# Tokens of a mixture-of-experts kernel gathered in 1 KB quarters and turned by VectorE in 32x32 blocks instead of by TensorE

## The reference

```python
DM, HID, EXPERTS, TOP_K = 1024, 512, 32, 2
x2 = rms_norm(h, ffn_norm[layer])                     # 512 x 1024
gp, gi = top_k(softmax(x2 @ w_r1 + b_r1), 1)          # one of 4 groups
ev, ei = top_k(fine logits of that group, 2)          # two of its 8 experts
gates = gp * softmax(ev)
for e in experts:                                     # w_gate, w_up: 1024 x 512, w_down: 512 x 1024
    y = (silu(x2[rows of e] @ w_gate[e]) * (x2[rows of e] @ w_up[e])) @ w_down[e]
    out[rows of e] += gate * y
h = h + out
```

## Time and profile before

| | us |
|---|---|
| median of 3 executions | 1716.42 (1715.44 to 1754.85) |
| profiled execution | 1716.88 |
| its span in the trace | 1715.0 |
| PE busy | 1654.8 (96%) |
| DVE busy | 743.6 (43%) |
| ACT busy | 327.6 (19%) |
| POOL busy | 76.7 (4%) |
| DMA queue 1, the weights | 455.11 MB, 67.7% of 16 engines' span |
| DMA queue 0, issued by POOL | 8.40 MB, 1.7% |

### The profile page before, as it was taken

How to read it: one execution, slowest core, us unless ns; L and a number is a source line. 1 busy time by engine, 2 the same in 40 slices (tenths; PEclk the granted TensorE clock), 3 DMA queues, 4 the chain that set the end, 5 groups by cost and what they waited for, 6 DMA issues and landing times.

```text
span 1715.0 us, 24253 instructions
## 1 busy us (share of the span) xinstructions
PE 1654.8 (96%) x10112; PEld 1088.4 (63%) x10119; DVE 743.6 (43%) x1281; ACT 327.6 (19%) x545; POOL 76.7 (4%) x76
## 2 busy tenths in 40 slices
PE   8999998999999999989999999999999999999998
PEld 6876686555555555547787787878655555555554
DVE  4899744333333333244453444445433333333333
ACT  4134621101001010123221222222100100000002
POOL 0030001000000000000000000000100000000000
PEclk9999999999999999999999999999999999999999
DMA  8212138999999999994222122127699999999995
GB/s 299 99 56 92 58 147 332 400 401 403 395 409 406 399 402 406 408 367 148 71 77 98 50 99 99 53 99 313 230 395 404 407 406 409 409 402 400 401 404 238
DMA packets 109553, 475.29 MB, mean 277 GB/s; under 512 B 10752, under 2 KB 23040, under 8 KB 76544
## 3 DMA queue, kind: packets, MB, share of 16 engines
q1 hardware_dynamic: 101120, 455.11, 67.7%
q0 software_dynamic: 5248, 8.40, 1.7%
q10 hardware_dynamic: 3072, 10.18, 1.5%
HBM read 476.27 MB, written 6.29 MB: 281 GB/s over the span
## 4 chain that ended last, share of the span: by engine, by line
PE 86%; DVE 8%; DMA 2%; issue 2%; ACT 1%; SPq 1%; DVEq 0%; POOLq 0%; ACTq 0%
PE psum L927 25%; PE psum L951 12%; PE psum L842 9%; PE psum L843 9%; PE psum L844 9%; PE psum L1038 8%; DVE h L2083 2%; PE psum L918 2%; PE psum L1336 2%; DVE xs L1747 2%; PE psum L936 2%; DMA raw<-in_odd_w_in 1%; PE psum L942 1%; DVE w_lo L666 1%; PE psum L1226 1%
## 5 line engine op out<-in xcount | busy, mean ns | idle before, releaser
L2083 DVE TENSOR_TENSOR h<-h,psum 128x512 f32<-128x512 f32 x240 | 154.2, 684 | 246.4 <-PE psum L1038 245.1
L666 DVE TENSOR_TENSOR w_lo<-raw,w_hi 128x2048 fp32r<-128x2048 f32 x46 | 105.4, 2291 | 202.1 <-ACT w_hi L660 202.1
L951 PE MATMUL psum<-raw,hidT 128*64 128x512 f32 x672 | 154.2, 601 | 1.1 <-ACT hidT L1541 1.1
L660 ACT ACTIVATE w_hi<-raw 128x2048 fp32r<-128x2048 f32 x46 | 88.1, 1914 | 335.9 <-PE psum L844 334.9
L842 PE MATMUL psum<-w_hi,uT_hi 128*128 128x512 f32 x352 | 139.5, 396 | 3.4 <-DVE h L2203 1.4
L1559 ACT ACTIVATE y_hi<-psum,rt 128x512 fp32r<-128x512 f32 x62 | 42.6, 687 | 506.9 <-PE psum L1038 366.5
L844 PE MATMUL psum<-w_lo,uT_hi 128*128 128x512 f32 x352 | 137.8, 392 | 0.0
L843 PE MATMUL psum<-w_hi,uT_lo 128*128 128x512 f32 x352 | 137.8, 391 | 0.0
L1038 PE MATMUL psum<-y_hi,to_token 64*128 64x512 f32 (+1 forms) x464 | 107.2, 444 | 20.6 <-DVE h L2083 17.8
L2321 POOL DMA_INDIRECT x_e<-xs_dram,index x64 | 60.3, 942 | 1464.5 <-PE psum L918 785.6
L2062 DVE SCALAR_TENSOR_TENSOR y_lo<-psum,rt,y_hi 128x512 fp32r<-128x512 f32 x66 | 49.2, 748 | 135.1 <-ACT y_hi L1559 135.0
(11 more groups left out here) (257 smaller groups left out, 2505.7 us busy)
## 6 DMA issues: line engine op xcount, KB each, us to landing
raw<-in_expert_w_down SPq DMA_DIRECT2D x84, 1024.0 KB, 23.7
raw<-in_expert_w_up SPq DMA_DIRECT2D x44, 1024.0 KB
free_a<-in_expert_w_gate SPq DMA_DIRECT2D x44, 1024.0 KB
in_pair<-in_expert_w_up SPq DMA_DIRECT2D x42, 1024.0 KB
in_uT<-in_expert_w_up SPq DMA_DIRECT2D x42, 1024.0 KB
free_b<-in_expert_w_gate SPq DMA_DIRECT2D x40, 1024.0 KB, 23.1
in_pair<-in_expert_w_down SPq DMA_DIRECT2D x40, 1024.0 KB, 23.2
xs<-in_expert_w_gate SPq DMA_DIRECT2D x40, 1024.0 KB, 23.7
```

The costliest lines, as they stand in the source:

```text
L660: nc.scalar.activation(part(w_hi[half]), half_of(n, half, by_columns), ACT.Copy).then_inc(hi_ok[half], 1)
L666: nc.vector.tensor_tensor(part(w_lo[half]), half_of(n, half, by_columns), part(w_hi[half]).bitcast(F32), ALU.subtract).then_inc(lo_ok[half ...
L951: mm = nc.tensor.matmul(psum[c * FIRST:(c + 1) * FIRST, bank], x[:, j % 2, (j // 2) * FIRST:(j // 2 + 1) * FIRST], w[:, j, c * 512:(c + 1) ...
L2083: ins = V.tensor_tensor(dst, dst, psum[:, SUM_BANKS[half]], ALU.add)
```

## The change

Tokens are gathered in quarters. x_e becomes [128, 2, 4, 256]: a set is 32 tokens, and quarter g of the width of token t of a set lies on partition 32 g + t. Each set is one indirect DMA of 128 rows of 1 KB (`sets_in_step`: 2 sets in a step, 4 in BIG), so a layer has 66 gathers and not 32. The indexes are quarter_of = 4 x token + (partition // 32).

For that the token list, which the router makes with slot s on partition s, has to be spread over four partition groups: `spread_tokens`, 16 small products with blocks of the identity into PSUM bank 7, and `spread_lists`, one DVE instruction that computes 4 x + group. Both run twice a layer, for the first four experts at the place of the list product and for the rest in step 0.

PE's transposes and DVE's copy go. In their place DVE turns x_e straight into xeT with one 32x32 block transpose a step (`turn_tokens`), which waits for the gather and for the up product of e-1. POOL waits for that (xT_ok) and not for PE. The waits of the sum tiles beside BIG go, the two warm runs of 12 and 14 products become adjacent, an index cast goes, and two copies for in_slot move behind the first turn.

```diff
-        x_e = place("x_e", [P, 2, DM], at=shared)
+        x_e = place("x_e", [P, 2, 4, DM // 4], at=shared)
+        xs_quarters = xs_dram.rearrange("t (g d) -> (t g) d", g=4)
...
+        def sets_in_step(e):
+            return rows_in_step(e) // 32
...
+                def spread_tokens(n):
+                    pe.wait_ge(tokens_ok, n)
+                    for s in range(4):
+                        for g in range(4):
+                            mm = nc.tensor.matmul(psum[32 * g:32 * g + 32, 7, s * EXPERTS:(s + 1) * EXPERTS],
+                                                  ident[:, 32 * s:32 * s + 32], slot_token, start=True, stop=True)
+                    mm.then_inc(spread, 1)
...
                 copied(pe, "pos", layer)
+                pe.wait_ge(bank_free[7], banks.before_experts[layer][7])
+                spread_tokens(2 * layer + 1)
                 warm(b, WARM[2])
...
-                pe.wait_ge(m.gathered[0], 16 * times(layer, 0))
-                transpose_tokens(m, x_e[:, 0], FIRST)
                 warm(2, WARM[4])
...
-                    if e == BIG - 1:
-                        pe.wait_ge(m.xT_ok, past + e + (q > 0) + 1)
...
                     sum_tile(e, 0)
-                    if e < STEPS - 1:
-                        pe.wait_ge(m.gathered[(e + 1) % 2], 16 * times(layer, e + 1))
-                        if e + 1 == BIG:
-                            pe.wait_ge(m.added, sum_no(layer, SUM_IN_STEP[e], 0) + 1)
-                        transpose_tokens(m, x_e[:, (e + 1) % 2], rows_in_step(e + 1))
+                    if not e:
+                        spread_tokens(2 * layer + 2)
                     sum_tile(e, 1)
...
-                make_lists(0, 1, link, index_ok)
+                t, p = make_rows(0, 1, link)
+                V.tensor_tensor(slot_token, t, p, ALU.add).then_inc(tokens_ok, 1)
+                spread_lists(2 * layer + 1, slice(0, EARLY))
...
+            def spread_lists(n, of):
+                dve.wait_ge(spread, n)
+                V.tensor_scalar(quarter_of[:, :, of], psum[:, 7, 0:4 * EXPERTS].rearrange("p (s e) -> p s e", s=4)[:, :, of], 4.0,
+                                small[:, 20:21], ALU.mult, ALU.add).then_inc(index_ok, 1)
+
+            def turn_tokens(m, layer, e):
+                past = STEPS * layer
+                s = sets_in_step(e)
+                dve.wait_ge(m.gathered[e % 2], gathered_at(layer, e))
+                if e > 1:
+                    dve.wait_ge(m.up_psum, past + e - 1)
+                V.transpose(xeT[:, e % 2, :, 0:32 * s].rearrange("p j (s t) -> p s j t", s=s),
+                            x_e[:, e % 2, 0:s].rearrange("p s (d j) -> p s j d", j=KC)).then_inc(m.xT_ok, 1)
...
-                copy_tokens(m, past + 1, xeT[:, 0], FIRST)
+                turn_tokens(m, layer, 0)
+                spread_lists(2 * layer + 2, ANY)
...
                     if e < STEPS - 1:
-                        copy_tokens(m, past + e + 2, xeT[:, (e + 1) % 2], rows_in_step(e + 1))
+                        turn_tokens(m, layer, e + 1)
...
-                G.indirect_dma_start(x_e[0:rows_in_step(e), b], None, xs_dram, bass.IndirectOffsetOnAxis(ap=rows_of(e), axis=0),
-                                     bounds_check=SEQ - 1, oob_is_err=False).then_inc(m.gathered[b], 16)
+                for s in range(sets_in_step(e)):
+                    G.indirect_dma_start(x_e[:, b, s], None, xs_quarters,
+                                         bass.IndirectOffsetOnAxis(ap=quarter_of[:, s, e:e + 1], axis=0),
+                                         bounds_check=4 * SEQ - 1, oob_is_err=False).then_inc(m.gathered[b], 16)
...
                 for e in range(STEPS - 2):
-                    pool.wait_ge(m.xT_psum, past + e + 1)
+                    pool.wait_ge(m.xT_ok, past + e + 1)
```

More of the change, by code:

```diff
@@ L128, in shape_constants @@
     small[:, 0:4] = np.arange(GROUPS, 0, -1)
+    small[:, 20] = p // 32
     small[:, 4:12] = np.arange(PER_GROUP, 0, -1)
@@ L401, in trunk_kernel @@
         oh_first = place("oh_first", [P, TOPK * TILES, P], F32R, at=token_at)
+        quarter_of = place("quarter_of", [P, 4, EXPERTS], U32, at=token_at + BLOCK - 4 * EXPERTS)
         y_hi.append(place("y_hi2", [P, 512], F32R, at=token_at))
@@ L547, in trunk_kernel @@
         gates_ok = sem("gates_ok")
+        tokens_ok = sem("tokens_ok")
+        spread = sem("spread")
         spill_ok = sem("spill_ok")
@@ L584, in turns_of, with gathered_at @@
             return range(2) if e == BIG else range(1)
-        def times(layer, e):
-            return layer * (STEPS // 2) + e // 2 + 1
+        def gathered_at(layer, e):
+            return 16 * sum(sets_in_step(k) for k in range(e % 2, e + 1, 2)) + \
+                16 * layer * sum(sets_in_step(k) for k in range(e % 2, STEPS, 2))
+        def sets_in_step(e):
+            return rows_in_step(e) // 32
         def last_tile(q):
@@ L1953, in route @@
                                 gates.unsqueeze(2).broadcast_to([P, TOPK * TILES, EXPERTS]), ALU.mult).then_inc(placed, 1)
-                dve.wait_ge(index_ok, 2 * layer + 1)
                 link(V.scalar_tensor_tensor(out=gate_late, in0=rank, scalar=float(FIRST), in1=gates, op0=ALU.is_ge,
@@ L1989, in spill @@
                 link(V.tensor_scalar(p, t, float(SEQ), -float(SEQ), ALU.is_ge, ALU.mult))
-                V.tensor_tensor(slot_token, t, p, ALU.add)
-                V.tensor_tensor(index[:, 0, ANY, 0], t[:, ANY], p[:, ANY], ALU.add).then_inc(index_ok, 1)
-                dve.wait_ge(index_ok, 2 * layer + 2)
+                V.tensor_tensor(slot_token, t, p, ALU.add).then_inc(tokens_ok, 1)
+                dve.wait_ge(tokens_ok, 2 * layer + 2)
                 place_gates()
@@ L2010, in place_gates @@
                 link(V.tensor_copy(out[:, BIG:BIG + 1], best[:, 1:2]))
-                V.tensor_copy(in_slot[FIRST:, :, 0:BIG], in_slot[0:FIRST, :, 0:BIG])
-                V.tensor_copy(in_slot[FIRST:, :, BIG + 1:], in_slot[0:FIRST, :, BIG + 1:]).then_inc(gates_ok, 1)
             def spill_gates(layer):
@@ L2024, in spill_gates, with make_rows @@
                 dve.wait_ge(spill_ok, layer + 1)
-            def make_lists(first, last, link, done):
+            def make_rows(first, last, link):
                 t, p = (a[:, first * EXPERTS:last * EXPERTS] for a in (table, prod_all))
@@ L2031, in make_lists @@
                 link(V.tensor_scalar(p, t, float(SEQ), -float(SEQ), ALU.is_ge, ALU.mult))
+                return t, p
+            def make_lists(first, last, link, done):
+                t, p = make_rows(first, last, link)
                 both_at = index[:, first:last].rearrange("p c e k -> p (c e) k")
@@ L2089, in moe @@
                 route(layer)
-                copy_tokens(m, past + 1, xeT[:, 0], FIRST)
+                turn_tokens(m, layer, 0)
+                spread_lists(2 * layer + 2, ANY)
+                V.tensor_copy(in_slot[FIRST:, :, 0:BIG], in_slot[0:FIRST, :, 0:BIG])
+                V.tensor_copy(in_slot[FIRST:, :, BIG + 1:], in_slot[0:FIRST, :, BIG + 1:]).then_inc(gates_ok, 1)
                 dve.wait_ge(gates_ok, layer + 1)
@@ L2313, in _ @@
             cosines("k")
-            def rows_of(e):
-                return index[0:rows_in_step(e), 0, e, 0:1]
             def gather(m, e, b):
-                G.indirect_dma_start(x_e[0:rows_in_step(e), b], None, xs_dram, bass.IndirectOffsetOnAxis(ap=rows_of(e), axis=0),
-                                     bounds_check=SEQ - 1, oob_is_err=False).then_inc(m.gathered[b], 16)
+                for s in range(sets_in_step(e)):
+                    G.indirect_dma_start(x_e[:, b, s], None, xs_quarters,
+                                         bass.IndirectOffsetOnAxis(ap=quarter_of[:, s, e:e + 1], axis=0),
+                                         bounds_check=4 * SEQ - 1, oob_is_err=False).then_inc(m.gathered[b], 16)
             def over_gather(m, c, e, n):
```

## The result

The changed kernel takes 1703.15 us, median of 7 executions, against 1716.42 us before: ratio 0.9923, interval 0.9911 to 0.9934. The forecast was 1704.9. The time came out as forecast; how it comes about did not, and most of what follows is on that.

A forecast was written before the change was run, and what follows sets the result against it. The prediction took the weight stream to set each layer's end, with PE's savings nearly all hidden. It summed 1716.9 + 11.7 (starts) - 1.5 (PE) - 22.2 (gathers) = 1704.9 us, own range 1697 to 1716, whole range 1690 to 1740.

The forecast's parts named there:

- likeliest case: The prediction's own forecast of 1704.9 us for the whole kernel, range 1697 to 1716, chance 0.60.
- What bounds the kernel: Expert loops: the weight stream uses up its lead by each layer's end, so PE savings inside bring about 2 us.
- The price of a gather: Expert loops: a step's gathers cost the weight stream 0.52 us in place of 0.89, -22.2 us over 60 steps.
- The row of BIG's gather: Rate of 418 GB/s around BIG's 128-row gather, nothing missing; new gathers were priced like it, by what they move.
- PE's part: Expert loops: removed transposes free 16.5 us a layer in steps without sums, 0 with sums; worth -1.5 us in all.
- The start: Start of each layer's experts: the spreads and DVE's wait for them delay gate 0 and the stream, +11.7 us together.
- DVE's chain: Start of each layer: DVE's part 4.8 us later, moving gate 0 by +4.8 in layer 1 and +2.9 in layer 0.
- The second spread: Step 0 of each layer: 3.7 us of spread for 1.1 of transposes idles the stream 2.0 us, +4.0 in all.
- DVE's block transpose: Each step on DVE: replaces the 0.69 us copy, bounded above by two products of 3.65 us, cost 0.
- a gather disturbs as before: Rival, expert loops: the 0.53 us disturbance stays, a step costs 1.05 us, 1737 us in all; chance 0.22.
- or twice: Rival, expert loops: each of a step's two DMAs disturbs, a step costs 1.58 us, 1768 us in all; chance 0.08.
- PE becomes the bound: Rival, expert loops: the stream gains so much that PE sets the time, 1697 us; chance 0.07.

The follow-up runs named there:

- e4: The kernel before with 1 of the 8 token transposes a step, gathers, copies and waits as before: 1716.97 us, ratio 1.0002.
- e6: The kernel before with each gather's index list over all 128 partitions, the same filled 4 KB rows: 1715.22 us, ratio 0.9997.
- e11: The changed kernel with every gather made twice, the second after the first has landed: 1734.67 us, ratio 1.0108.
- e10: The changed kernel with the sum tiles of the step ahead of BIG again waiting for BIG's turned tokens: 1711.19 us, ratio 0.9968.
- e7: The changed kernel with hid's transposes moved into the gate product and the second sum tile into the down product: 1698.30 us, ratio 0.9896.
- e8: e7 without loading the last quarter of each down block, chunk 2 used twice instead: 1678.88 and 1679.48 us in the two executions that count.
- e9: The kernel before with index lists over 128 partitions and the second sum tile in the middle of the down product: 1704.90 us, ratio 0.9939.

## Why the prediction was right in time, and where it was wrong

The time: 1704.9 forecast, 1703.15 measured, in the likeliest case's own range of 1697 to 1716. Point by point:

- **What bounds the kernel.** "The lead is as good as used up, so PE time saved inside the loop is worth about 2 us": e4 shows it, with a ratio of 1.0002. Its other half failed: "what the stream gains or loses counts in full". The stream was ahead, by those 2 us at the last block and by 1.3 and 0.4 us at the closest, so PE set the pace. e6 gave the stream 5 and 8 us more of lead there and no time came off. The step that failed is to treat the runner that is 2 us ahead as the one that sets the end; the gain is PE's own, up to the stream's gain and its small lead, and I had added the whole of the stream's gain to what was left of PE's.
- **The price of a gather**, 0.52 us: 0.49 by the rate, 0.53 to 0.57 by doubling (e11). The row of BIG's gather had been the right one to price by, since what counts is the list of 128 (e6: 0.58 us). But the terms behind the 0.52 were not met: 288 packets a step were counted, 0.40 us of quarters and 0.12 of small ones, and there are 96, which take 0.37 us, with 0.12 of loss beside them. That the sum came so close is in part luck. The -22.2 us that followed were there as capacity of the stream (0.89 - 0.49 = 0.40 a step, 24 us) and only the 16.2 us that PE could use of them became time.
- **PE's part**, 16.5 us a layer. In the steps without sums it was some 0.43 us and not 1.03, and in 14 steps and not 16, so 6.1: the transposes had hidden ACT's copy of hidT, for which the prediction has no term. The last line of the earlier trace rows shows that wait, 0.47 us in the step that has no transposes. When work leaves the path, what is late next has to be named; here it was hidT. In the steps with sums it was 0, as said: from tile to tile 2.67 us before and 2.68 after.
- **BIG's waits** stood in the change's description and in no term of the sum. They were 4.1 and 2.5 us, in layer 0 with a lower clock behind them, and e10, with one wait of another length, lost 8 us in two layers.
- **The start**, +11.7. The spread took 0.46 us, below the lower end of 1.3: I priced a product by the router's with 128 columns, and took the row's price rather than a part of it. DVE's chain was +3.3 us in layer 1 and +0.4 in layer 0, and in layer 1 only 0.67 of it is DVE's wait for the spread. Most of it is slot_gate: the 27 warm products ahead of it stand behind the spread, start 1.6 us after the list's copy where they had started before it, and took 4.79 us at a granted clock of 0.64 where they had taken 3.12 at 1.00. So slot_gate started at 1210.03, where the gates were ready at 1207.2. Gate 0 in layer 0 took 5.36 us for 4.33, as forecast (5.10). The second spread is 0.6 us shorter than the transposes were, so the +4.0 was -1.2. In all +3 to +4.
- **DVE's block transpose**: 1.10 us for 128 x 512, inside the bounds, hidden. It is 0.4 us longer than the copy.
- **The sum.** Forecast +11.7 at the starts and -23.7 in the loops, measured +3 to +4 and -16.2: the start was too dear by 8, the loops gained 7.5 less, and the errors nearly cancelled, so that the time came within 2 us is luck. As a forecast of the time it was right, as a forecast of the mechanism it was right in what relieves the stream and wrong in what then sets the pace.
- **The rivals.** That a gather disturbs as before, or twice, fell by the 413 GB/s. That PE becomes the bound was given 0.07 and a time of 1697; it is what happened in layer 1 and at all but one block of layer 0, at 1703, since PE gained 9.0 and 7.2 us in the loops and not 16.5 each.

## What to carry to other kernels

Where two runners end within a few us of each other, price both in full and take the later one: relieving either alone gave 0.0% here (e4, e6), both together 0.8%. Relieving PE once more gave 5 us and then met the stream (e7); with less stream as well it gave 24 (e8). And look for the closest block, not only at the last: in e9 the lead ran out 6 blocks before it. Before an instruction on the path is removed, look at what other engines do under it; its gain is its duration less the wait that it hid. And of a list of edits, a wait that disappears in one step of 32 deserves a price as much as the work that gives the change its name.

## What the runs showed of the hardware that I had not expected

- An indirect gather with a list of 64 rows costs the full stream beside it 0.89 us, of which its own packets are 0.46 (2.9% of 440 us over 28); a list of 128, with the same filled rows and more packets, costs 0.58, with 0.39 of its own (403 against 411 GB/s over 440 us, 306 against 407 in 3 us around one gather of each).
- Gathers of 1 KB rows in lists of 128 gave hardly any packets of 1 KB: 96 packets a step for 128 filled rows and as many empty ones, and 16 packets of 512 B to 2 KB in 440 us.
- 16 float32 products of 32 columns that write four groups of 32 partitions took 0.46 us; 16 products of 128 columns of the router 3.68.
- 8 transposes of 64 x 128 took 1.09 us reading every eighth column, 0.65 to 0.71 reading neighbouring ones; that the columns' distance is the cause was not tried by itself.
- A wait of 3.7 us on PE was followed by a down product of 5.62 us in place of 3.65. Two waits of 1.47 and 1.41 us were followed by one of 4.42 us in layer 0 and of 3.65, at full clock, in layer 1; one of 1.47 us, nearly always by 3.65 and once by 4.54. What a wait costs can be more than its length, and the same wait need not cost the same.
